# Difference attention's first units scored inside the last key projection, from buffers of their own; next projection's weights split two units sooner

## The reference

```python
h = rmsnorm(x, norm_mix[l])
aq, ak, av, bq, bk, bv, cin = split_last(h @ w_in[l], IN_SIZES)
...
def block(args):
    qblk, i = args
    s = jnp.einsum('bqhcd,bkhcd->bhcqk', qblk, k).astype(f32) * (DIFF_QK_DIM ** -0.5)
    ...
    s = s - slopes[None, :, None, None, None] * dist[None, None, None]
    p = jax.nn.softmax(s, axis=-1)
    a = p[:, :, 0] - lam * p[:, :, 1]
    return jnp.einsum('bhqk,bkhe->bqhe', a.astype(v.dtype), v)
```

## Time and profile before

| what | value |
|---|---|
| median of 3 runs | 1897.2 us (1892.85 to 1897.43) |
| the profiled execution | 1889.26 us, span 1887.5 us |
| busy share of TensorE, VectorE, ScalarE, GpSimd | 91%, 39%, 35%, 29% |
| mean granted clock of TensorE | 0.96 of full speed |
| job 5 (last key projection) | 137.2 to 158.9 us of the span |
| difference attention | 158.9 to 336.5 us |
| jobs 6 and 7 | 342.2 to 394.9 us |

### The profile page before, as it was taken

One profiled execution on the slowest core, in us unless ns is written; L12 is line 12 of the kernel. 1 busy time (PEld: TensorE's weight loads), 2 busy tenths in 40 slices (PEclk: granted clock), 3 DMA queues, 4 the chain that ended last, 5 costly groups with the idle time before them and its releaser, 6 DMA issues.

```text
span 1887.5 us, 32560 instructions
## 1 busy us (share of the span) xinstructions
PE 1714.2 (91%) x13937; PEld 1429.4 (76%) x13937; DVE 728.1 (39%) x1209; ACT 651.3 (35%) x1218; POOL 544.8 (29%) x498
## 2 busy tenths in 40 slices
PE   6998999799766982989999899999999999999998
PEld 5886878688554761777997687888888888888886
DVE  3104888043175557455232263131133033213316
ACT  4224888223256433433234374211111121211212
POOL 4222662221034325325234102222222222222220
PEclk9998999899878995999999999999999999999999
DMA  5110000121000000002413101211111111111112
GB/s 185 51 60 1 1 1 1 40 61 34 17 1 6 4 4 0 4 4 75 160 49 97 34 1 51 57 50 41 55 50 46 45 51 51 44 56 48 43 45 95
DMA packets 60176, 81.20 MB, mean 43 GB/s; under 512 B 4626, under 2 KB 47792, under 8 KB 60032
## 3 DMA queue, kind: packets, MB, share of 16 engines
q1 hardware_dynamic: 59088, 76.60, 12.9%
q0 software_dynamic: 944, 2.52, 0.5%
HBM read 74.90 MB, written 4.19 MB: 42 GB/s over the span
## 4 chain that ended last, share of the span: by engine, by line
PE 81%; DVE 10%; ACT 5%; issue 2%; DMA 1%; POOL 1%; SPq 0%; DVEq 0%; ACTq 0%
PE PS L1540 13%; PE PS L1543 13%; PE PS L1541 13%; PE PS L1793 7%; PE PS L2137 4%; PE PS L2135 4%; PE PS L2136 4%; PE PS L1553 3%; PE PS L1555 3%; PE PS L1554 3%; PE PS L1651 3%; PE PS L1685 2%; PE PS L1857 2%; PE PS L1677 1%; PE PS L2056 1%
## 5 line engine op out<-in xcount | busy, mean ns | idle before, releaser
L428 POOL TENSOR_TENSOR WL<-RAW,WH 128x512 fp32r<-128x512 f32 x224 | 305.7, 1374 | 912.5 <-ACT WH L590 912.5
L1540 PE MATMUL PS<-HH,WH 128*128 128x512 f32 x1040 | 407.2, 391 | 9.5 <-POOL WL L428 8.1
L1541 PE MATMUL PS<-HL,WH 128*128 128x512 f32 x1040 | 406.3, 391 | 0.0
L590 ACT ACTIVATE WH<-RAW 128x512 fp32r<-128x512 f32 x224 | 138.7, 631 | 595.2 <-PE PS L1543 294.6
L1543 PE MATMUL PS<-HH,WL 128*128 128x512 f32 x1040 | 321.9, 391 | 0.0
L1540 PEld LDWEIGHTS PS<-HH,WH 128*128 128x128 f32 x1040 | 196.4, 189 | 50.7 <-issue 8.4
L1543 PEld LDWEIGHTS PS<-HH,WL 128*128 128x128 f32 x1040 | 196.2, 189 | 41.0
L1541 PEld LDWEIGHTS PS<-HL,WH 128*128 128x128 f32 x1040 | 196.3, 189 | 40.6
L1490 DVE TENSOR_TENSOR FU<-PS,ACTB 128x512 f32<-128x512 f32 x44 | 27.3, 684 | 456.9 <-PE PS L1543 456.9
L2135 PE MATMUL PS<-WH,AH 128*128 128x512 f32 x352 | 136.9, 389 | 0.0
L2136 PE MATMUL PS<-WL,AH 128*128 128x512 f32 x352 | 136.9, 389 | 0.0
(11 more groups left out here) (317 smaller groups left out, 2781.7 us busy)
## 6 DMA issues: line engine op xcount, KB each, us to landing
RAW<-in_ffn_w_gu SPq DMA_DIRECT2D x88, 256.0 KB, 2.8
RAW<-in_w_in SPq DMA_DIRECT2D x48, 256.0 KB, 2.8
RAW<-in_ffn_w_down SPq DMA_DIRECT2D x44, 256.0 KB, 2.6
XT<-in_x SPq DMA_DIRECT2D x8, 512.0 KB, 5.5
RAW<-in_w_out SPq DMA_DIRECT2D x16, 256.0 KB, 2.7
X<-in_x SPq DMA_DIRECT2D x8, 512.0 KB, 8.2
RAW<-in_x_wkv SPq DMA_DIRECT2D x16, 256.0 KB, 2.6
out_x<-FO SPq DMA_DIRECT2D x8, 512.0 KB, 2.6
```

What stands on the lines that cost most here:

```text
L428: pool.tensor_tensor(w_low, RAW[:, p % NRAW], w_high.bitcast(F32), ALU.subtract).then_inc(w_lo, 1)
L590: act.activation(split_at(p)[0], RAW[:, p % NRAW], ACT.Copy).then_inc(w_hi, 1)
L1540: pe.matmul(where(ct, i), wh[:, k, c], ah(kt)[:, t0:t0 + n], start=first and starts(ct, i), stop=False, skip_group_check=True)
L1541: pe.matmul(where(ct, i), wh[:, k, c], al(kt)[:, t0:t0 + n], start=False, stop=False, skip_group_check=True)
```

## The change

Units 0 and 1 get buffers of their own outside the weight slots: KS0 holds the keys of head 0, QS0 the queries of units 0 and 1, QS1 those of units 2 and 3. Their memory is that of MIX for heads 1 to 3 and of OB's second half, which are written later. Staging for them waits for the evacuation of jobs 2 and 4 (`job_evac` 12 and 20) and no longer for the end of job 5. TensorE makes the scores of unit 0 behind the second quarter of job 5 and those of unit 1 behind the third. On ScalarE the key copies and the four exponentials of units 0 and 1 stand ahead of the evacuation of job 5, and the first transposes wait for two banks of that evacuation (`job_evac` 22). GpSimd stages units 2 and 3 into QS1 before it waits for the end of job 5, and units 4 and 5 into QST behind it.

At the other end, ScalarE makes the high parts of pieces 24 to 26 in unit 30, GpSimd makes the low parts of pieces 24 to 29 before it waits for head 3, and `d_head(3)` stands behind the third quarter of job 6.

```diff
+        KS0 = at("KS0", 112, [2, T], F32R)
+        QS0, QS1 = at("QS0", 120, [2, 2, 2 * P], F32R), at("QS1", 203.5, [2, 2, 2 * P], F32R)
...
+        def keys_of(h):
+            return KST[:, h % 2] if h else KS0
+        def queries_of(n):
+            return QST[:, n % 2] if n >= 2 else (QS0, QS1)[n]
...
# GpSimd
-            pool.wait_ge(w_used, 24)
-            pool.wait_ge(w_lo, 24)
-            pool.wait_ge(job_evac, 24)
...
+            pool.wait_ge(w_lo, 24)
+            pool.wait_ge(job_evac, 12)
+            stage_queries(1)
+            pool.wait_ge(w_used, 24)
+            pool.wait_ge(w_lo, 24)
+            pool.wait_ge(job_evac, 24)
             for h in range(4):
-                for g in range(0 if h else 1, 4):
+                for g in range(0 if h else 2, 4):
...
-            for p in range(24, 28):
+            for p in range(24, 30):
                 lo(p)
             pool.wait_ge(hm_evac, 8)
...
# ScalarE
             def k_first_parts(h):
+                if h == 1:
+                    act.wait_ge(w_lo, 24)
+                    act.wait_ge(w_used, 24)
...
+                act.wait_ge(job_evac, 24 if h else 20)
...
+            for j in range(2, 6):
+                hi(min(4 * j + 10, 24))
+                if j == 5:
+                    k_first_parts(0)
+                    act.wait_ge(lam_s, 1)
+                    act.activation(LAM[:, 0:2], LAM[:, 0:2], ACT.Exp).then_inc(lam_e, 1)
+                    d_exp(0)
+                    d_exp(1)
+                evac_proj(j)
...
+                if u == 30:
+                    act.wait_ge(qk_done, 64)
+                    hi(24 + NRAW)
...
-            act.wait_ge(qk_done, 64)
             hi(24 + NW)
...
# VectorE
-            dve.wait_ge(w_used, 24)
-            dve.wait_ge(w_lo, 24)
+            dve.wait_ge(job_evac, 20)
...
# TensorE
+            def first_scores(q):
+                if q == 1:
+                    pe.wait_ge(job_evac, 20)
+                    d_scores(0)
+                if q == 2:
+                    d_scores(1)
+            for j in range(2, 6):
+                proj(j, first_scores if j == 5 else None)
...
+                if u == 0:
+                    pe.wait_ge(job_evac, 22)
...
+            def last_head(q):
+                if q == 2:
+                    d_head(3)
             for j in range(6, NJ):
-                proj(j)
-                if j == 6:
-                    d_head(3)
+                if j == 7:
                     pe.wait_ge(hm_evac, 8)
+                proj(j, last_head if j == 6 else None)
```

More of the change, by code:

```diff
@@ L468, in stage_keys, with stage_queries @@
                 ins.then_inc(k_staged, 1)
+            def stage_queries(n):
+                q = queries_of(n)
+                for c in (1, 0):
+                    same, other = slice(64 * c, 64 * c + 64), slice(64 - 64 * c, 128 - 64 * c)
+                    src = BQ[same, n // 4, 2 * P * (n % 4):2 * P * (n % 4 + 1)]
+                    link(stage(q[same, 0, c, :], q[same, 1, c, :], src))
+                    for part in range(2):
+                        ins = pool.tensor_copy(q[other, part, c, :], q[same, part, c, :].bitcast(F32))
+                ins.then_inc(q_staged, 1)
+            pool.wait_ge(w_lo, 24)
[4 more added lines that the diff above has]
+            pool.wait_ge(job_evac, 24)
             for h in range(4):
-                for g in range(0 if h else 1, 4):
+                for g in range(0 if h else 2, 4):
                     n = 4 * h + g
[L473 to L481, removed]
+                    pool.wait_ge(qk_done, 4 * (n - 1))
+                    stage_queries(n)
                     if g == 3 and h < 3:
                         stage_keys(h + 1)
-            for p in range(24, 28):
+            for p in range(24, 30):
                 lo(p)
@@ L488, in _ @@
             pool.memset(CIN[:, :, T + 1:T + 2], 0.0).then_inc(pads, 1)
-            for p in range(28, 4 * NJ):
+            for p in range(30, 4 * NJ):
                 lo(p)
@@ L668, in evac_proj @@
                                        ACT.Copy).then_inc(job_evac, 1)
-            for j in range(2, 6):
-                hi(min(4 * j + 10, 24))
-                evac_proj(j)
             def k_first_parts(h):
+                if h == 1:
+                    act.wait_ge(w_lo, 24)
+                    act.wait_ge(w_used, 24)
                 if h >= 2:
                     act.wait_ge(qk_done, 16 * (h - 1))
+                act.wait_ge(job_evac, 24 if h else 20)
                 for c in (1, 0):
                     rows = slice(64 * c, 64 * c + 64)
[L680 to L686, removed]
+                    act.activation(keys_of(h)[rows, c, :], BK[rows, h, :], ACT.Copy).then_inc(k_first, 1)
             def d_exp(u):
@@ L710, in d_evac @@
                     act.activation(MIX[:, h, b * 512:b * 512 + 512], PS[:, 7, :], ACT.Copy, scale=SUBC).then_inc(hm_evac, 1)
-            d_exp(0)
-            d_exp(1)
+            for j in range(2, 6):
[7 more added lines that the diff above has]
+                evac_proj(j)
             for u in range(32):
@@ L1063, in _ @@
                 src = BQ[same, 0, 0:2 * P]
[L1064 to L1068, removed]
+                link(dve.tensor_copy(QS0[same, 0, c, :], src))
+                dve.tensor_copy(QS0[other, 0, c, :], QS0[same, 0, c, :].bitcast(F32))
+                link(TT(QS0[same, 1, c, :], src, QS0[same, 0, c, :].bitcast(F32), ALU.subtract))
+                dve.tensor_copy(QS0[other, 1, c, :], QS0[same, 1, c, :].bitcast(F32))
                 dve.wait_ge(k_first, i + 1)
-                TT(KST[other, 0, c, :], BK[same, 0, :], KST[same, 0, c, :].bitcast(F32), ALU.subtract).then_inc(k_second, 1)
+                TT(KS0[other, c, :], BK[same, 0, :], KS0[same, c, :].bitcast(F32), ALU.subtract).then_inc(k_second, 1)
             dve.wait_ge(lam_e, 1)
@@ L1612, in _, with proj @@
             pe.transpose(PS[:, 3, 0:42], VROWS, ID[0:42, 0:42]).then_inc(vec_t, 1)
-            def proj(j):
+            def proj(j, after=None):
                 if j == 2:
@@ L1628, in proj @@
                 else:
-                    feature_job(4, hh, hl, lambda ct, i: PS[:, bank + 2 * ct + i, :])
-            for j in range(2, 6):
-                proj(j)
-            pe.wait_ge(job_evac, 24)
+                    feature_job(4, hh, hl, lambda ct, i: PS[:, bank + 2 * ct + i, :], after=after)
             def d_scores(u, maps=(0, 1)):
@@ L1650, in d_scores @@
                         for half in range(2):
-                            mm = pe.matmul(PS[:, 2 * c + half, :], QST[:, u // 2 % 2, part, c, P * (u % 2):P * (u % 2) + P],
-                                           KST[:, h % 2, c, 512 * half:512 * half + 512], start=part == 0, stop=part == 1, skip_group_check=True)
+                            mm = pe.matmul(PS[:, 2 * c + half, :], queries_of(u // 2)[:, part, c, P * (u % 2):P * (u % 2) + P],
+                                           keys_of(h)[:, c, 512 * half:512 * half + 512], start=part == 0, stop=part == 1, skip_group_check=True)
                     mm.then_inc(qk_done, 1)
@@ L1663, in d_head @@
                     mm.then_inc(ht_done, 1)
-            d_scores(0)
-            d_scores(1)
+            def first_scores(q):
[6 more added lines that the diff above has]
+                proj(j, first_scores if j == 5 else None)
             for u in range(32):
```

## The result

The changed kernel takes 1862.7 us, median of 4 runs (1860.6 to 1868.4), against 1897.3 us, median of 4 (1892.9 to 1897.9) for the kernel before. The ratio on record is 0.9848, 95% interval 0.9825 to 0.9871; it is an estimate of its own and not the quotient of the two medians, which is 0.9817. So this timing gives two sizes of the gain, 34.7 us by the medians and 28.8 us by the ratio. Timed a second time the ratio was 0.9859 (0.9838 to 0.9879). The profiled execution has a span of 1860.2 us in place of 1887.5, 27.3 less.

The account below looks back on a forecast made before the run. TensorE, 91% busy, was taken as the bound, losing time to waits and slow clock where attention meets the projections. Front 14.3 plus rear 12.9 gave 27.2 us; 1897.2 - 27.2 = 1870.0, range 1863 to 1880.

Parts of the forecast that it names:

- step (a): Front, units 0 and 1: VectorE's staging takes 6.71 us beside job 5, ends 2.0 us before TensorE needs it, costs nothing.
- (b): Front: sixteen score matmuls move into job 5 and lengthen it by 3.7 us, between 3.6 and 4.0.
- (c): Front: softmax of units 0 and 1 runs beside job 5's last two quarters, ending 2.3 us before ScalarE's evacuation is due.
- (d): Front: unit 1's value product starts 7.9 us after job 5 ends, before 26.0; with the added scores, 14.3 us gained.
- GpSimd's staging of units 4 and 5: Front, after job 5's evacuation: takes 5.0 us and ends 2.6 us before unit 4's scores are due, so covered.
- Rear: From attention's last value product through jobs 6 and 7: waits and slow-clock time go, 5.77 + 2.88 + 2.28 + 1.99 = 12.9 us.
- the slow start of job 6: Job 6 took 24.64 us, 2.88 above 21.76, because its start ran at clock 0.50; this goes if the clock holds.
- The term of 1.99 for job 7: Job 7 took 23.75 us, 1.99 above 21.76, booked on the slow clock and expected to go.
- The first term: TensorE's 5.77 us wait before job 6 for the low part of weight piece 24, expected to go.
- Rival A: The clock doesn't hold at both seams: gain only 17.7 us, time 1879.5; chance 0.10.
- Rival C: Attention units 2 to 31: GpSimd's staging sets the pace, pairs take 12 us, not 9.2; time 1909; chance 0.03.
- D: The early start is worth nothing, as attention or the projections behind meet a later common wait; time 1897; chance 0.04.

## Why the prediction was right

The prediction was 1870.0 us, from a gain of 27.2, range 1863 to 1880. The median of the first timing, 1862.7, lies just outside the lower end that the text gives; the second timing's 1865.4 lies inside. The mechanism is the one predicted, and the sum is borne out to a fraction of a microsecond against the profile that it was worked out from. That the two spans differ by 27.3 is partly luck: the seams give 14.6 + 12.9 = 27.5, the later work gives 1.6 more, and the stretch ahead of job 5 takes back 1.8. And that profile is at the slow end for its seams: the same front took 45.7 in two of four profiles, and the same rear 59.8 in one of two, so with these other readings the seams' gain would be 24.8 us. Step by step:

- **Front, step (a), staging ready:** I said 6.71 us for VectorE's part and 2.0 of cover. It took 5.04 with GpSimd idle beside it, so the cover was 3.5 (146.15 to 149.69). Its outputs also lie in other buffers than before, and no run parts the two. The price was too high, without effect, as the step is covered.
- **(b), sixteen scores inside job 5:** 3.7. From the evacuation of job 4 to that of job 5 are 164.40 - 139.01 = 25.39 us, so 3.63 above 21.76.
- **(c), exponentials:** I gave ScalarE 2.3 us of cover; its row shows 2.69. The experiment that takes this cover away costs 5.2.
- **(d), from the end of job 5 to unit 1:** 7.9 predicted; job 5 ends at 163.75 + 0.61 = 164.36, and 172.13 - 164.36 = 7.8 measured. VectorE's combination for unit 1 took 1.47 us and ended at 170.22, 0.1 ahead of the transposes at 170.32, where I had 0.45 of cover: VectorE nearly set the pace here. The gain of the front is 47.7 - 33.1 = 14.6, predicted 14.3.
- **GpSimd's staging of units 4 and 5,** cover 2.6 predicted; it ends at 171.61 and unit 4's scores start at 173.91, 2.3 later, with no wait.
- **Rear:** predicted 12.9, measured 60.5 - 47.6 = 12.9. The parts are confirmed by experiment, though not to the last quarter of a microsecond. The wait and the slow start of job 6 are 8.9 when split out alone (8.65 in the sum), the slow start by itself 2.75 (2.88), and the order behind it 4.0 (4.27). The term of 1.99 for job 7 is 0.25 too large: it runs from TensorE's start to ScalarE's row at 394.94, while TensorE starts the job behind at 394.69. The first term is 0.25 too small: the start of job 6 moved from 7.83 to 1.81 us behind that of the last value product, 6.02 in place of 5.77. The two cancel. The transposes cost their 0.78 of waiting, under the 1 us that I gave.
- **Rival A, the clock:** it held, 1.00 at both seams, through the waits of 0.27 and 0.78 that were left. The experiments show that it was worth naming: when a wait of 2.19 or 6.46 us came back, the clock fell with it. **Rival C** didn't come about: the attention stretch stayed at 149.5. **D** neither.

What is off is the distance between medians, 34.7 in the first timing, against 27.3 between the profiles. The step for that was "I set the gain against the median, the profile ran 7.9 below it". It took for granted that the changed kernel's profile would lie as far below its own median; it lies 0.7 below. The forecast of 1870.0 lies 7.3 us above the first timing's median; that the range nearly reaches it, and holds the second timing's, is owed to the range's width and not to that step. The profiles show how such distances can come about. The work behind job 7 is the same in all ten profiles, and takes 1488.1 to 1500.9 us. For the changed kernel's two profiles:

```profile
369.20:1860.20 1491.00, 1366.90 (x12048) 1140.59 (x12046) 544.50 (x915) 447.30 (x854) 394.66 (x310) 0.95 0.14 43
...
367.30:1868.20 1500.90, 1372.28 (x12048) 1144.75 (x12046) 543.79 (x915) 447.27 (x854) 394.01 (x310) 0.95 0.14 42
```

The same 12048 matmuls are busy for 5.4 us more in the second, by their rows; VectorE and ScalarE are not. Matched matmul by matmul, the second profile falls behind mainly in two places, and in both the granted clock is lower. Here are these stretches, between the same matmuls, first in the first profile and behind the mark in the other:

```profile
478.40:498.60 20.20, 17.69 (x81) 12.89 (x80) 2.18 (x4) 11.30 (x12) 0.00 (x0) 0.75 0.01 2
815.50:839.90 24.40, 20.02 (x219) 13.69 (x216) 12.07 (x18) 9.63 (x11) 12.45 (x6) 0.79 0.08 23
...
476.10:501.20 25.10, 20.80 (x82) 15.96 (x81) 2.59 (x6) 11.30 (x12) 0.00 (x0) 0.66 0.00 1
819.20:847.00 27.80, 23.41 (x219) 16.48 (x214) 12.14 (x18) 9.79 (x13) 14.07 (x7) 0.68 0.07 21
```

They take 4.9 and 3.4 us more, 8.3 of the 9.9. That the clock is at its lower level for longer in some executions fits most of this spread; no run sets the clock there, so it is not shown as the whole cause. Over the ten profiles the time at the lower level behind job 7 goes from 113 to 143 us, and the shortest and the longest work go with its ends, but 133 us of it go with 1491.0 as well as with 1494.2. What makes up the 7.9 between profile and median in the first timing stays open, since those runs left no trace.

## What to carry to other kernels

When two stages meet on one engine, look for which buffer ties the second's first step to the first's last. Here 16 KiB a partition, free at that time since their owners write later, take 14.6 us out of the front in this pair of profiles, by letting staging and softmax run beside a projection. Price a wait of TensorE with the slow clock behind it, and count what comes after a removed wait: at one head change the wait of 1.39 us for ScalarE hid a VectorE instruction that took 2.86 us in place of 1.28. Check also each queue in between: half of the front's gain, by the trace, hangs on GpSimd making one staging ahead of its wait.

## What the runs showed of the hardware

- Filling a wait of 5.8 us with matmuls whose result nobody reads kept the granted clock at 1.00 and made the job behind it 2.75 us faster (24.64 to 21.89), at no cost, since the time was idle anyway.
- The clock's answer to the same wait isn't the same each time: the front of the kernel before took 47.7 and 47.8 us in two profiles and 45.7 in two others, with waits of 5.76 and of 1.20 or 1.21 ahead of unit 0's scores in all. In the stretch behind, the granted clock was 0.81 from 176 to 185 us in the first profile, and 1.00 from 175.4 to 184.4 in the one with the filled wait.
- VectorE's ten staging instructions took 6.71 us with GpSimd's staging beside them and 5.04 with GpSimd idle, and a combination of 1.28 us took 2.88 beside a GpSimd subtraction.
